# One product of each expert combine put behind the next transposes, the last down product and combine split by column halves, and the square root's table loaded earlier, in a one-core decoder step

## What is computed

```python
def hier_moe(h, ...):
    ...
    for e in range(N_EXPERTS):
        hid = silu(t @ w_gate[e]) * (t @ w_up[e])
        acc = acc + combine[:, e:e + 1] * (hid @ w_down[e])
...
y_prompt = rmsnorm(xp, ln_final)
y_sample = rmsnorm(xs, ln_final)
```

## Time and profile before

| | |
|---|---|
| median of 3 runs | 818.65 us (816.97 to 820.39) |
| the profiled execution's own time | 818.35 us |
| its span in the trace | 816.6 us |
| PE busy | 770.8 us (94%) |
| DVE, ACT, POOL busy | 268.6, 158.6, 139.1 us |
| HBM read | 246.87 MB |

### The profile page before, as it was taken

One profiled execution on the slowest core, in us unless ns is written; L12 is line 12 of the kernel. 1 busy time (PEld: TensorE's weight loads), 2 busy tenths in 40 slices (PEclk: granted clock), 3 DMA queues, 4 the chain that ended last, 5 costly groups with the idle time before them and its releaser, 6 DMA issues.

```text
span 816.6 us, 8712 instructions
## 1 busy us (share of the span) xinstructions
PE 770.8 (94%) x3488; PEld 374.3 (46%) x3488; DVE 268.6 (33%) x614; ACT 158.6 (19%) x313; POOL 139.1 (17%) x167
## 2 busy tenths in 40 slices
PE   4999999989999999889999999999999999999996
PEld 3777677758743334544333333333333333333332
DVE  2059999995356632531111011101101110110101
ACT  3211121224541101300210121011111111210214
POOL 2069899702002000010000000000000000000000
PEclk9999999999999999989999999999999999999999
DMA  9894200040608189989999999999999999999992
GB/s 276 305 342 171 105 20 0 2 110 26 182 26 266 39 283 327 429 319 426 428 426 427 428 424 426 428 427 426 428 426 426 426 428 426 428 427 426 428 395 68
DMA packets 51256, 249.58 MB, mean 306 GB/s; under 512 B 6966, under 2 KB 24406, under 8 KB 38655
## 3 DMA queue, kind: packets, MB, share of 16 engines
q1 hardware_dynamic: 45540, 243.54, 74.4%
q10 hardware_dynamic: 3147, 2.67, 1.1%
q0 software_dynamic: 2528, 2.79, 1.1%
HBM read 246.87 MB, written 8.61 MB: 313 GB/s over the span
## 4 chain that ended last, share of the span: by engine, by line
PE 69%; DVE 5%; ACT 3%; issue 2%; DMA 0%; DVEq 0%; ACTq 0%; POOLq 0%
PE bank L1177 27%; PE bank L1200 14%; PE bank L1051 9%; PE bank L1218 8%; DVE region_a L1569 2%; PE bank L1189 1%; PE bank L1024 1%; PE bank L1015 1%; DVE bank L1570 1%; ACT region_a L1496 1%; PE bank L788 1%; PE bank L1040 1%; PE bank L885 1%; PE bank L1178 1%; DVE bank L1599 1%
## 5 line engine op out<-in xcount | busy, mean ns | idle before, releaser
L788 PE MATMUL bank<-region_a,ring 128*128 128x320 f32 x576 | 158.8, 436 | 0.5 <-DVE region_a L1569 0.5
L1569 DVE TENSOR_TENSOR region_a<-region_a,bank 64x512 f32<-64x512 f32 (+1 forms) x33 | 22.5, 681 | 379.8 <-ACT region_a L1496 379.7
L1178 PE MATMUL bank<-ring,zz 128*64 128x512 f32 x304 | 135.8, 601 | 0.0
L788 PEld LDWEIGHTS bank<-region_a,ring 128*128 128x128 f32 x576 | 109.6, 192 | 46.7 <-issue 2.2
L1177 PE MATMUL bank<-ring,zz 128*64 128x512 f32 x272 | 121.8, 602 | 3.2 <-issue 2.6
L1570 DVE SCALAR_TENSOR_TENSOR bank<-region_a,par,bank 128x256 f32<-128x256 f32 x232 | 91.2, 479 | 0.0
L744 POOL DMA_INDIRECT region_a<-hn_scratch,region_a x16 | 15.9, 995 | 374.3 <-PE bank L1160 357.9
L1218 PE MATMUL bank<-zz,masks 128*128 128x512 f32 (+1 forms) x192 | 74.7, 602 | 2.1 <-ACT zz L1502 2.1
L1051 PE MATMUL bank<-ring,x_v_y 128*128 128x512 f32 (+1 forms) x192 | 74.1, 606 | 0.8 <-DVE x_v_y L1569 0.8
L1496 ACT ACTIVATE region_a<-bank 64x512 f32<-64x512 f32 x32 | 18.9, 589 | 278.7 <-PE bank L1178 278.7
L1177 PEld LDWEIGHTS bank<-ring,zz 128*64 128x64 f32 x272 | 36.3, 138 | 78.4 <-issue 77.8
(11 more groups left out here) (310 smaller groups left out, 793.9 us busy)
## 6 DMA issues: line engine op xcount, KB each, us to landing
ring<-in_expert_w_up SPq DMA_DIRECT2D x19, 2048.0 KB, 27.3
ring<-in_expert_w_down SPq DMA_DIRECT2D x18, 2048.0 KB, 35.5
ring<-in_expert_w_gate SPq DMA_DIRECT2D x16, 2048.0 KB, 31.6
ring<-in_w_in SPq DMA_DIRECT2D x9, 2048.0 KB, 20.3
x_v_y<-in_expert_w_down SPq DMA_DIRECT2D x7, 2048.0 KB, 27.0
x_v_y<-in_expert_w_gate SPq DMA_DIRECT2D x5, 2048.0 KB, 33.7
ring<-in_w_out SPq DMA_DIRECT2D x4, 2048.0 KB, 9.1
xcx<-in_expert_w_gate SPq DMA_DIRECT2D x4, 2048.0 KB, 32.5
```

The lines of the kernel that those rows point to most:

```text
L788: ins = pe.matmul(pt[0:m, 0:T], w[:, k, :], ht[:, k, :], start=k == 0, stop=k == KD - 1)
L1178: ins = pe.matmul(to[CAP:P, :], x[:, k, :], wu[:, FE * k:FE * k + FE], **st)
L1569: tt_ = lambda out, a, b, op: dve.tensor_tensor(out, a, b, op)
```

## The change

1. The combine of pair i-2 is split. Five products (`combine_most`) stay between the two experts' gate and up, and the sixth (tile 1, second half; `combine_rest`) goes behind the eight transposes and ahead of the down products. In pair 15, which has no such transposes, it goes between gate and up and the downs.
2. The down product of expert 31 is made by output halves (`down_half`): first columns 0 to 511, as two stacked blocks of 256 columns, then columns 512 to 1023, in a bank of its own. ACT copies each half with two copies of 64x256 (`half_back`).
3. The last combine takes tiles 0 and 1 first, the first column half of both, then the second half of both, then the sample tile. The final norm, the scaling and the output follow that order, so the sample tile is last. The second half of the sample rows is sent from ACT's queue.
4. The instruction that calls up the square root's table, a square root of one column, goes from behind the branch to a place ahead of the copies of experts 30 and 31.

```diff
@@ SP
-            sp_.wait_ge(S("y_final"), 1)
-            for q in range(2):
-                sp_.dma_start(few[:, 512 * q:512 * q + 512], y_few[TS * q:TS * q + TS, :]).then_inc(S("y_out"), 16)
             for r in range(2):
                 for q in range(2):
-                    sp_.wait_ge(S("y_final"), 2 + 2 * r + q)
+                    sp_.wait_ge(S("y_final"), 1 + 2 * r + q)
...
+            sp_.wait_ge(S("y_final"), 5)
+            sp_.dma_start(few[:, 0:512], y_few[0:TS, :]).then_inc(S("y_out"), 16)
@@ PE
+            def down_half(to, x, wd, q):
+                for k in range(4):
+                    for h in range(2):
+                        c0 = D * k + 512 * q + 256 * h
+                        ins = pe.matmul(to[CAP * h:CAP * h + CAP, 0:256], x[:, k, :], wd[:, c0:c0 + 256],
+                                        start=k == 0, stop=k == 3)
+                return ins
...
+            PARTS = [(2, 0), (2, 1), (0, 0), (0, 1), (1, 0), (1, 1)]
...
-            def combine(i):
+            def combine_most(i):
                 pe.wait_ge(S("places"), i + 1)
                 pe.wait_ge(S("yo"), 2 * i + 2)
-                to_tokens(back[i % 2], yo_of).then_inc(S("added"), 1)
+                to_tokens(back[i % 2], yo_of, PARTS[:-1])
+
+            def combine_rest(i):
+                to_tokens(back[i % 2], yo_of, PARTS[-1:]).then_inc(S("added"), 1)
...
                     if i >= 2 and e % 2:
-                        combine(i - 2)
+                        combine_most(i - 2)
...
                     for h in range(2):
                         tokens_T(i + 1, h)
+                if i >= 2:
+                    combine_rest(i - 2)
                 if i:
                     expert_down(2 * i - 2)
                     expert_down(2 * i - 1)
                 hidden_T(i)
-            combine(NE // 2 - 2)
+            combine_most(NE // 2 - 2)
+            combine_rest(NE // 2 - 2)
             over = pe.value_load(mcount[0:1, 0:1], min_val=0, max_val=T)
             expert_down(NE - 2)
-            expert_down(NE - 1)
+            w_down = expert_landed(pe, 2, NE - 1)
+            down_half(job_free(pe, "down", NE - 1), hidt[:, :, own_half[1]], w_down, 0).then_inc(S("dn_half"), 1)
+            pe.wait_ge(S("hidt"), NE // 2)
+            down_half(job_bank("hidden", NE // 2 - 1), hidt[:, :, own_half[1]], w_down, 1).then_inc(S("dn_done"), 1)
...
             pe.wait_ge(S("places"), NE // 2)
+            pe.wait_ge(S("yo"), NE - 1)
+            pe.wait_ge(S("yo_half"), 1)
+            for r in range(2):
+                to_tile(back[1], yo_of, r, 0, end=True).then_inc(S("summed"), 1)
             pe.wait_ge(S("yo"), NE)
-            to_tokens(back[1], yo_of, end=True)
+            for r in range(2):
+                to_tile(back[1], yo_of, r, 1, end=True).then_inc(S("summed"), 1)
+            to_tile(back[1], yo_of, 2, 0, end=True)
+            to_tile(back[1], yo_of, 2, 1, end=True).then_inc(S("summed"), 1)
@@ ACT
             wait(act, S("added"), NE // 2 - 1)
+            act.activation(ssq[:, 6:7], ssq[:, 7:8], ACT.Sqrt)
             rows_back(NE - 2)
-            rows_back(NE - 1)
+            def half_back(pt, q):
+                for h in range(2):
+                    ins = act.activation(yo[own_half[1], 512 * q + 256 * h:512 * q + 256 * h + 256],
+                                         pt[CAP * h:CAP * h + CAP, 0:256], ACT.Copy)
+                return ins
+            act.wait_ge(S("dn_half"), 1)
+            half_back(job_bank("down", NE - 1), 0).then_inc(S("yo_half"), 1)
+            act.wait_ge(S("dn_done"), NE)
+            half_back(job_bank("hidden", NE // 2 - 1), 1).then_inc(S("yo"), 1)
             over = act.value_load(mcount[0:1, 0:1], min_val=0, max_val=T)
             with act.If(over > CAP):
...
-            act.activation(ssq[:, 6:7], ssq[:, 7:8], ACT.Sqrt)
-
...
-            square3(4, 0, ssq[:, 2:3])
-            part(rst[0:TS, 6:7], ssq[TS:P, 2:3], slice(TS, P))
-            part(rst[TS:P, 6:7], ssq[0:TS, 2:3], slice(0, TS))
-            root(rst[:, 2:3], ssq[:, 2:3], rst[:, 6:7], 2)
-            square3(0, 1, ssq[:, 0:1])
+            square3(0, 0, ssq[:, 0:1])
             part(rst[:, 7:8], ssq[:, 0:1], slice(0, P))
-            square3(1, 2, ssq[:, 3:4])
-            root(rst[:, 0:1], ssq[:, 3:4], rst[:, 7:8], 3)
-            square3(2, 3, ssq[:, 1:2])
+            square3(2, 1, ssq[:, 1:2])
             part(ssq[:, 5:6], ssq[:, 1:2], slice(0, P))
-            square3(3, 4, ssq[:, 4:5])
-            root(rst[:, 1:2], ssq[:, 4:5], ssq[:, 5:6], 4)
+            square3(1, 2, ssq[:, 3:4])
+            root(rst[:, 0:1], ssq[:, 3:4], rst[:, 7:8], 1)
+            square3(3, 3, ssq[:, 4:5])
+            root(rst[:, 1:2], ssq[:, 4:5], ssq[:, 5:6], 2)
+            square3(4, 4, ssq[:, 2:3])
+            part(rst[0:TS, 6:7], ssq[TS:P, 2:3], slice(TS, P))
+            part(rst[TS:P, 6:7], ssq[0:TS, 2:3], slice(0, TS))
+            root(rst[:, 2:3], ssq[:, 2:3], rst[:, 6:7], 4)
+            act.wait_ge(S("y_final"), 5)
+            act.dma_start(O["y_sample"].rearrange("b t d -> (b t) d")[:, 512:D], y_few[TS:P, :])\
+                .then_inc(S("y_out"), 16)
@@ DVE
-            inverse3(0, 2)
-            scaled(y_few, 4, 2, gfin_few)
             for r in range(2):
-                inverse3(r + 1, r)
+                inverse3(r, r)
                 for q in range(2):
                     scaled(y_rows[:, r, 512 * q:512 * q + 512], 2 * r + q, r, gfin[:, 512 * q:512 * q + 512])
+            inverse3(2, 2)
+            scaled(y_few, 4, 2, gfin_few)
```

More of the change, by code:

```diff
@@ L1207, in expert_down, with to_tile, to_tokens @@
                 down(job_free(pe, "down", e), hidt[:, :, own_half[e % 2]], w_down).then_inc(S("dn_done"), 1)
[L1209 to L1220, removed]
+            def to_tile(rows, of, r, q, end=False):
+                t0, n = TILES[r]
+                dst = acc[2 * r + q][:, :] if r < 2 else acc[4][TS * q:TS * q + TS, :]
+                return pe.matmul(dst, rows[:, t0:t0 + n], of[q][0:rows.shape[0], :], start=False, stop=end)
+            PARTS = [(2, 0), (2, 1), (0, 0), (0, 1), (1, 0), (1, 1)]
+            def to_tokens(rows, of, parts=PARTS):
+                for r, q in parts:
+                    ins = to_tile(rows, of, r, q)
                 return ins
             yo_of = [yo[:, 512 * q:512 * q + 512] for q in range(2)]
-            def combine(i):
+            def combine_most(i):
                 pe.wait_ge(S("places"), i + 1)
                 pe.wait_ge(S("yo"), 2 * i + 2)
-                to_tokens(back[i % 2], yo_of).then_inc(S("added"), 1)
+                to_tokens(back[i % 2], yo_of, PARTS[:-1])
+            def combine_rest(i):
+                to_tokens(back[i % 2], yo_of, PARTS[-1:]).then_inc(S("added"), 1)
             pe.wait_ge(S("gath"), 16)
@@ L1541, in root @@
                 act.activation(to, of, ACT.Sqrt, scale=1.0 / D, bias=rest).then_inc(S("rt3"), 1)
-            square3(4, 0, ssq[:, 2:3])
+            square3(0, 0, ssq[:, 0:1])
+            part(rst[:, 7:8], ssq[:, 0:1], slice(0, P))
+            square3(2, 1, ssq[:, 1:2])
+            part(ssq[:, 5:6], ssq[:, 1:2], slice(0, P))
+            square3(1, 2, ssq[:, 3:4])
[3 more added lines that the diff above has]
+            square3(4, 4, ssq[:, 2:3])
             part(rst[0:TS, 6:7], ssq[TS:P, 2:3], slice(TS, P))
             part(rst[TS:P, 6:7], ssq[0:TS, 2:3], slice(0, TS))
-            root(rst[:, 2:3], ssq[:, 2:3], rst[:, 6:7], 2)
-            square3(0, 1, ssq[:, 0:1])
-            part(rst[:, 7:8], ssq[:, 0:1], slice(0, P))
-            square3(1, 2, ssq[:, 3:4])
-            root(rst[:, 0:1], ssq[:, 3:4], rst[:, 7:8], 3)
-            square3(2, 3, ssq[:, 1:2])
-            part(ssq[:, 5:6], ssq[:, 1:2], slice(0, P))
-            square3(3, 4, ssq[:, 4:5])
-            root(rst[:, 1:2], ssq[:, 4:5], ssq[:, 5:6], 4)
+            root(rst[:, 2:3], ssq[:, 2:3], rst[:, 6:7], 4)
+            act.wait_ge(S("y_final"), 5)
+            act.dma_start(O["y_sample"].rearrange("b t d -> (b t) d")[:, 512:D], y_few[TS:P, :])\
+                .then_inc(S("y_out"), 16)
             act.wait_ge(S("keep_out"), 16)
```

## The result

| | before | changed |
|---|---|---|
| median | 818.89 us (816.97 to 821.45, 20 runs) | 821.92 us (818.37 to 824.51, 20 runs) |
| profiled execution, span | 818.35, 816.6 us | 820.15, 818.3 us |
| experts begin (first gate product) | 358.46 us | 358.53 us |
| pair 15 begins | 765.87 us | 765.80 us |
| from pair 15's start to the end of the span | 50.73 us | 52.50 us |

The ratio is 1.003 with a 95% interval of 1.0021 to 1.004: slower, but by less than the 0.5% (4.1 us) that the prediction set as the least difference to be told from no change. The ratio is not that of the two medians. In microseconds it is 2.5 (1.7 to 3.3), the medians are 3.0 apart, and the two profiled executions 1.8. The table says where the 1.8 lie: the pairs are not a tenth of a microsecond faster, and the end is 1.77 us longer.

A forecast was written before the change was run, and what follows sets the result against it. The stream of weights was taken to bound the kernel up to 765.87 us, then PE, then ACT and DVE. Profiled 818.35 plus 0 in the pairs and 1.6 at the end (pair 15's 0.3 included) gave 820.0 us, range 817.8 to 822.2.

The forecast's parts named there:

- rival 1: At the head of pair 15 the clock falls after idle time, costing 1.7 us: 821.7 us; chance 0.21.
- rival 2: Behind the branch one table load serves squares and roots, first root 1.3 us sooner: 818.7 us; chance 0.08.
- the early load: At the end, the first table load behind the branch starts at 805.56 us, the early bound; 805.8 was taken.
- The moved product: Pairs 2 to 14: PE needs 0.42 us less in each, 5.5 in all, costed at nothing because the weights cover it.
- The sign given for it: No idle time ahead of the downs, and 2 us or more of it at the heads of pairs 11 to 14.
- Pair 15, +0.3: In pair 15 the moved product stands alone between narrow forms, adding 0.3 us, bounded by 0 and 0.5.
- Halves at no cost: Expert 31's down product in halves streams the same number of columns: 0 us, up to +1.0 if loads did not pair.
- Two loads on the path: Behind the branch, one table load ahead of the first square and one ahead of the first root, 1.28 us each.
- DVE ends last: At the end, DVE's five scalings follow the first root at 811.2 us, take 4.2 us and end at 815.4.
- The rule of a drain behind each load: Adds some 1.38 us to each load's 1.28, for an end 2.8 us later, 822.8; the prediction rejected it.
- a gain over before of 1.0: At the end, with neither load there, DVE's last scaling would end near 812.8 us and the kernel gain 1.0 us.
- rival 3: The pairs do get shorter: weights land sooner and 5.5 us reach the end, 814.5 us; chance 0.03.

The follow-up runs named there:

- the product alone: The kernel before with only the sixth product of each combine moved (part 1 of the change): median 820.26 us, ratio 1.0003.
- six, five and two additional products: Extra 320-column products on PE at pair heads: six on the changed kernel, 826.08 us; five and two on changed end, no load, combines as before, 820.42 and 818.81 us.
- the end alone: The changed kernel with all six products of each combine back where they were (parts 2 to 4 without part 1): median 821.87 us, ratio 1.0025.

## Why the prediction was right, and where it was not

The time of 821.92 us lies in the range, near its upper end. By the profiled execution the sum was nearly exact: a span of 818.2 was forecast and 818.3 measured. In the median there was luck: 821.92 is nearer to rival 1's 821.7 than to 820.0, though neither profile of the changed kernel shows that rival's fall at pair 15, and the repeat gave 822.30, just above the range's 822.2. The range's lower end does not follow from its terms either: rival 2 with the early load and no cost in pair 15 is 818.7 - 0.2 - 0.3 = 818.2, not 817.8.

- **The moved product is worth nothing: right.** A pair took 27.31 us, 0.49 less than before (0.42 forecast), and the product alone and the changed kernel begin pair 15 407.3 to 407.6 us after the experts, the kernel before 407.4. The sign given for it held only in part: idle time of 2 us or more was named for pairs 11 to 14, and pair 13 had 0.97, because the fall at pair 12 had used up some of it.
- **Pair 15, +0.3: right.** The product alone made the end 0.32 longer, and the combines put back made it 0.31 shorter (52.50 against 52.19).
- **Halves at no cost: right.** The two halves took 3.62 us, expert 31's share of the 7.09 before is 3.55; each pair of copies 0.77.
- **Two loads on the path: right,** and shown by taking one and both away. Together they cost 2.4 us. The prediction's "instead of none" is the aim of the change; the kernel before had one there.
- **DVE ends last: right.** The first root ended at 811.16 (811.2 forecast), DVE at 815.24 (815.4). From there to the end of the span it took 3.1 us, against 2.49 before and 2.8 in the sum. This and DVE's 0.16 are two small errors that cancelled. Without both loads a gain over before of 1.0 was named; the ends differ by 0.66, since the longer tail stays.
- **The rule of a drain behind each load.** The Trainium skill (ScalarE: Activation LUTs, What ACT_TABLE_LOAD costs) adds some 1.38 us to each. Here ACT went on 0.02 us after a load of 1.28, and both loads together gave back 2.43 us; the trace does not agree.
- **The median: mis-sized.** The weak step is the last of the sum, "820.0": it took the profiled execution for the middle. The medians lie 1.8 and 1.9 us above the changed kernel's two profiles, and 0.5 above the one of before.
- **Rival 1, what decides a fall: wrong.** "It decides where an idle time of 2.0 us is enough, between 1.60 and 2.44" does not hold. In eleven profiles (all but those with six, five and two additional products) there are 27 waits of 1.9 us or more at the heads of pairs 11 to 15; 11 of them were followed by a fall and 16 not, among these waits of 3.18, 3.11 and 2.87 us, while one of 1.96 was. After 1.67 us or less none was. The price was right (1.66 to 1.7 us). That a fall at 11 to 14 is hidden held in every profile without additional products, and the one fall seen at 15 was not hidden.
- **Rivals 2 and 3: did not come.** The changed kernel's trace has both loads behind the last copy, and pair 15 begins at 765.80 us, not sooner. Rival 2's state of one load was made by hand (one load behind the branch): its end is 51.52 us.

What stays open is whether there is more behind the median than the end explains (3.0 against 1.77). By the ratios the two sets of runs of the changed kernel are 2.5 us (1.7 to 3.3) and 2.0 us (0.8 to 3.1) over before, and 1.77 lies in both intervals: a surplus is not shown. The medians can overstate it, because the times fall into groups. In the repeat no run lies between 820.39 and 822.07; four are below and eight above, and both profiled executions (820.15 and 820.39) belong to the lower runs. The mean granted clock goes with it: 0.981 to 0.982 in those four, 0.975 to 0.980 in the eight. So the slower runs had more time at 1.2 GHz; where, no profile of one of them shows.

Falls at pair 15 would do it, and one such fall was seen, in another kernel. For them speaks that no run of the kernel before passed 821.72 us; 1.77 more is 823.5, and three of the 32 runs of the changed kernel are above that, while the end alone, whose PE has less idle time, has none above 821.72 + 1.46 in twelve. Against them speaks that the five profiles with the moved product and no additional ones show waits of 1.98 to 2.02 us at pair 15 and no fall, that the end alone has as large a median, and that two additional products changed nothing. Late starts of the experts, of which the profiles show some, are as good a cause. Medians of 12 runs with a spread of 3 to 5 us don't tell these apart.

## What to carry to other kernels

Ask first whether the engine you relieve waits for a stream that is full: here 13 times 0.49 us less on PE turned into 6.0 us more waiting and nothing else. After moving a function to another place, read the compiled order for table loads, above all behind a branch in whose untaken path another table is used; here a root at the end of that path took both loads away. And compare stages from a common event to the end of the span: two pairs of single profiles gave the same end within 0.1 us, while the times of one kernel spread over 3 to 6 us, and a median among grouped times can jump from one group to the other.

## What the runs showed of the hardware

- A table load ahead of a square did not serve the root that followed, and the one ahead of a root served both: two loads of 1.28 us against one, or none where the same table was in place on both ways out of the branch.
- After idle times of 1.96 to 2.54 us at a pair's head PE sometimes ran at 1.2 GHz (a window with a granted clock of 0.50) and lost 1.66 to 1.7 us, and sometimes not, even after 3.18 us.
- Two executions of the same instructions began the experts 3.4 us apart; 1.8 of it was there at 43 us, behind a stretch with a granted clock of 0.84 against 1.00.
- A product of 320 fp32 columns with 128-column weights took 0.57 us; in the trace it is two rows, and I had counted one.
